# A two-layer backbone on one core: token-side norm behind the feed-forward, six modulation tiles moved to the router, pair parameters a step early

## What is computed

```
x = x + gate * rms_norm(sublayer(modulate(x, norm_pre, shift, scale)), norm_post)
```

## Time and profile before

| | |
|---|---|
| median of 3 runs | 1936.82 us (1935.96 to 1938.35) |
| profiled execution | 1934.04 us |
| its span | 1932.3 us |
| mean granted TensorE clock | 0.954 |
| busy: PE, VectorE, ScalarE, GpSimd | 1767.5, 1284.7, 985.6, 132.3 us |
| HBM read, written | 438.99 MB, 2.62 MB |

### The profile page before, as it was taken

One profiled execution on the slowest core, in us unless ns is written; L12 is line 12 of the kernel. 1 busy time (PEld: TensorE's weight loads), 2 busy tenths in 40 slices (PEclk: granted clock), 3 DMA queues, 4 the chain that ended last, 5 costly groups with the idle time before them and its releaser, 6 DMA issues.

```text
span 1932.3 us, 32651 instructions
## 1 busy us (share of the span) xinstructions
PE 1767.5 (91%) x11466; PEld 1430.8 (74%) x11466; DVE 1284.7 (66%) x1889; ACT 985.6 (51%) x1356; POOL 132.3 (7%) x208
## 2 busy tenths in 40 slices
PE   4989999977979998898669999999999999999997
PEld 2757777756768884797558788887878787878785
DVE  4345666665255551322379898989888898989897
ACT  1322222221234443122248787877777777878684
POOL 0134333330000000110000000000000000000000
PEclk8889999988989998899869999999999999999999
DMA  9531111020755437433339898988989797979790
GB/s 402 211 142 41 41 41 41 3 90 17 316 228 183 152 135 290 152 135 135 155 119 370 302 366 315 369 333 344 351 326 370 295 372 298 379 303 367 307 351 22
DMA packets 61367, 442.86 MB, mean 229 GB/s; under 512 B 7008, under 2 KB 8160, under 8 KB 10080
## 3 DMA queue, kind: packets, MB, share of 16 engines
q1 hardware_dynamic: 59184, 437.81, 59.3%
q10 hardware_dynamic: 1584, 2.79, 0.4%
q0 software_dynamic: 512, 1.05, 0.2%
HBM read 438.99 MB, written 2.62 MB: 229 GB/s over the span
## 4 chain that ended last, share of the span: by engine, by line
PE 81%; DVE 8%; issue 4%; DMA 3%; ACT 2%; POOL 1%; DVEq 0%; ACTq 0%; POOLq 0%; SPq 0%
PE PS L865 33%; PE PS L894 17%; PE PS L616 4%; PE PS L953 3%; PE PS L593 3%; PE PS L1044 2%; PE PS L699 2%; PE PS L1067 2%; PE PS L573 2%; PE PS L557 2%; DMA MIX<-w_mod 2%; PE PS L958 1%; PE PS L882 1%; DVE LO L1501 1%; PE PS L679 1%
## 5 line engine op out<-in xcount | busy, mean ns | idle before, releaser
L1501 DVE TENSOR_TENSOR LO<-W,HI 128x1024 fp32r<-128x1024 f32 x662 | 781.9, 1222 | 111.7 <-ACT HI L1101 65.2
L1101 ACT ACTIVATE HI<-W 128x1024 fp32r<-128x1024 f32 x662 | 689.7, 1062 | 137.4 <-PE PS L865 77.5
L865 PE MATMUL PS<-HI,XHI 128*128 128x512 f32 x970 | 393.5, 406 | 16.4 <-ACT XHI L1300 14.1
L865 PE MATMUL PS<-HI,XLO 128*128 128x512 f32 x970 | 380.6, 392 | 0.0
L865 PE MATMUL PS<-LO,XHI 128*128 128x512 f32 x970 | 294.8, 393 | 9.1 <-DVE LO L1501 8.5
L865 PEld LDWEIGHTS PS<-HI,XHI 128*128 128x128 f32 x970 | 183.1, 189 | 55.6 <-issue 15.8
L865 PEld LDWEIGHTS PS<-LO,XHI 128*128 128x128 f32 x970 | 181.3, 188 | 55.6 <-DVE LO L1501 16.3
L865 PEld LDWEIGHTS PS<-HI,XLO 128*128 128x128 f32 x970 | 183.5, 189 | 34.9
L894 PE MATMUL PS<-HI,HHI 128*128 128x512 f32 x484 | 188.9, 390 | 1.5 <-ACT HHI L1277 1.5
L894 PE MATMUL PS<-HI,HLO 128*128 128x512 f32 x484 | 188.3, 389 | 0.0
L894 PE MATMUL PS<-LO,HHI 128*128 128x512 f32 x484 | 145.5, 389 | 0.0
(11 more groups left out here) (285 smaller groups left out, 2160.0 us busy)
## 6 DMA issues: line engine op xcount, KB each, us to landing
W<-w_exp SPq DMA_DIRECT2D x298, 1024.0 KB, 6.9
W<-w_ffn SPq DMA_DIRECT2D x33, 1024.0 KB, 4.9
W<-w_mod SPq DMA_DIRECT2D x32, 1024.0 KB, 13.0
MIX<-w_mod SPq DMA_DIRECT2D x16, 1024.0 KB, 16.8
W<-w_rkv SPq DMA_DIRECT2D x8, 1792.0 KB, 8.2
W<-w_qkv SPq DMA_DIRECT2D x8, 1536.0 KB, 7.9
W<-w_o SPq DMA_DIRECT2D x1, 4096.0 KB, 12.0
W<-w_o SPq DMA_DIRECT2D x1, 3072.0 KB, 11.1
```

The source lines that it names most:

```text
L865: last = mm(PS[2 * (s % 2) + g], x[:, 2 * n + k, T * g:T * g + T], w[:, 512 * k:512 * k + 512], start=(n == 0 and k == 0 and i == 0 and le ...
L1101: fn(HI[:, u % NBUF], raw_unit(phase, u), ACT.Copy).then_inc(hi_ready, 1)
L1501: tt(LO[:, u % NBUF], raw_unit(phase, u), HI[:, u % NBUF].bitcast(F32), ALU.subtract)\
```

## The change

1. Layer 1's tiles 6 to 11 leave the stretch before attention. Their 12 blocks go to five buffers in MIX; SP issues five when the feed-forward is through and seven at the router, in front of the expert loads that need the output weights' place. TensorE runs tiles 6 to 9 in front of `norm_sum(7)` and tiles 10, 11 behind it.
2. Behind the feed-forward the post norm is made with tokens on partitions: ScalarE squares the four banks with a running sum (NSUM), makes a root for two columns (NROOT), VectorE a reciprocal; ScalarE and VectorE scale the banks into YNAT; TensorE turns them; VectorE adds them to XT straight from PSUM with the gain. `norm_sum(4)` is gone.
3. `norm_pre` works and signals by quarters of two chunks (`h_quarter`), for the feed-forward also the low part; attention's first product and the router's turning wait for quarters.
4. In the RWKV steps PP is copied at the end of the step before; TensorE runs `right_side` ahead of `prep_coef`, and `prep_hat` behind `solve0`; VectorE masks one gram in front of the hat copy. The last two steps of VectorE's loop are written out.
5. In an expert job one split stands ahead of the gathered copies on ScalarE and VectorE.

```diff
 # TensorE, mix_step
                 if ahead is not None:
                     prep_gate(ahead[2])
+                right_side(c, p)
                 if prep is not None:
                     prep_coef(prep[0])
-                    prep_hat(prep[0])
-                right_side(c, p)
                 for n, f in enumerate((solve0, solve1, solve2)):
                     if prep is not None:
                         gram(n % 2, prep[0], prep[1], 1 + n // 2)
                     for e in range(2):
                         f(e, c, p)
+                    if prep is not None and n == 0:
+                        prep_hat(prep[0])
...
 # VectorE
-            def prep_params(c, r, p):
+            def prep_params(c, p):
+                cs = slice(c, c + 1) if isinstance(c, int) else bass.ds(c, 1)
+                if not isinstance(c, int) or c >= 2:
+                    dve.wait_ge(prep_pool, 3 * (c - 2) + 3)
+                    dve.wait_ge(prep_act, 4 * (c - 2) + 2)
+                nc.vector.tensor_copy(PP[p].unsqueeze(1), PAIR[:, cs]).then_inc(prep_dve, 1)
...
                     prep_bonus(*prep[:2])
+                    gram(0, prep[0], 1 - p, 1)
                     prep_hat(*prep[:2])
-                    gram(0, prep[0], 1 - p, 1)
+                    if more:
+                        prep_params(prep[0] + 1, p)
                     gram(1, prep[0], 1 - p, 1)
...
+            def norm_pre(n, l, k, split_low=False):
+                dve.wait_ge(root_ready, seq(n))
                 order(nc.vector.reciprocal(RSTD, RMS))
-                order(tt(B[1], XT, RSTD.unsqueeze(1).to_broadcast([P, C, TT]), ALU.mult))
-                norm_shift(l, k)
+                for b in range(4):
+                    part = B[1][:, 2 * b:2 * b + 2]
+                    order(tt(part, XT[:, 2 * b:2 * b + 2], RSTD.unsqueeze(1).to_broadcast([P, 2, TT]), ALU.mult))
+                    norm_shift(l, k, range(2 * b, 2 * b + 2)).then_inc(h_quarter, 1)
+                    if split_low and b:
+                        low_quarter(b - 1)
+                if split_low:
+                    low_quarter(3)
...
 # SP
-            for late in range(MOD_LOADS - 2 * EARLY):
-                if late < 7:
-                    sp.wait_ge(lo_ready, UNITS["ffn"] + 2 * (FFN_LOADS - 6 + late))
-                else:
-                    sp.wait_ge(mod_used, MOD_LOADS + 2 * EARLY + late - 6)
+            for late in range(2 * (MIDDLE - EARLY)):
+                sp.wait_ge(lo_ready, UNITS["ffn"] + 2 * (FFN_LOADS - 6 + late))
                 load("late", late, a["w_mod"][1, 2 * EARLY + late])
-                if late == 8:
-                    attention_start()
-            sp.wait_ge(mod_used, 2 * MOD_LOADS)
+            attention_start()
+            sp.wait_ge(lo_ready, UNITS["exp"])
             sp.dma_start(W[:, WO1:W_COLS], a["w_o"][1]).then_inc(wo_full[1], 16)
+            sp.wait_ge(lo_used, UNITS["exp"])
+            def last_tiles(lo, hi):
+                for late in range(lo, hi):
+                    if late >= LATE:
+                        sp.wait_ge(mod_used, MOD_LOADS + 2 * MIDDLE + late - LATE + 1)
+                    m = 2 * MIDDLE + late
+                    sp.dma_start(mod_block(1, m), a["w_mod"][1, m]).then_inc(late_full[late % LATE], 16)
+            last_tiles(0, LATE)
...
                 if slot("exp", m) == WO1 // LOAD:
+                    last_tiles(LATE, MOD_LOADS - 2 * MIDDLE)
                     sp.wait_ge(wo_psum[1], 4)
...
 # ScalarE, behind the feed-forward
-                    last = fn(YNAT[:, g, 512 * half:512 * half + 512], PS[4 + 2 * g + half], ACT.Copy)
-            last.then_inc(yn_sbuf, 1)
+                    last = fn(flat[0][...], PS[4 + 2 * g + half], ACT.Square, accum_out=NSUM[:, g, half:half + 1])
+            last.then_inc(nsum_act, 1)
+            act.wait_ge(nsum_dve, 1)
+            fn(NROOT, NSUM[:, :, 0], ACT.Sqrt, scale=1.0 / D, bias=BIASES[:, 0:1]).then_inc(nsum_act, 1)
+            act.wait_ge(nsum_dve, 2)
+            for half in range(2):
+                fn(YNAT[:, 0, 512 * half:512 * half + 512], PS[4 + half], ACT.Copy, scale=NROOT[:, 0:1])\
+                    .then_inc(yn_act, 1)
...
 # ScalarE and VectorE, expert job
                 hidden(NS - 1)
+                split("exp", 2 * FFN_LOADS, j)
                 gathered(j + 1)
-                split("exp", 2 * FFN_LOADS, j)
                 split("exp", 2 * FFN_LOADS + 1, j)
```

More of the change, by code:

```diff
@@ L206, in mod_block @@
         def mod_block(l, m):
-            if l == 0 and m >= 2 * EARLY:
-                at = (m - 2 * EARLY) % LATE * LOAD
+            first = 2 * (MIDDLE if l else EARLY)
+            if m >= first:
+                at = (m - first) % LATE * LOAD
                 return MIX[:, at:at + LOAD]
@@ L363, in build @@
         loads, had = {}, [0] * RING
-        for name, n in (("mod0", 2 * EARLY), ("mod1", 2 * EARLY), ("ffn", FFN_LOADS), ("late", MOD_LOADS - 2 * EARLY),
+        for name, n in (("mod0", 2 * EARLY), ("mod1", 2 * EARLY), ("ffn", FFN_LOADS), ("late", 2 * (MIDDLE - EARLY)),
                         ("exp", 0)):
@@ L377, in mod_arrived @@
         def mod_arrived(eng, l, m):
-            late = m - 2 * EARLY
-            if late < 0:
+            late = m - 2 * (MIDDLE if l else EARLY)
+            if m < 2 * EARLY:
                 arrived(eng, f"mod{l}", m)
-            elif l:
-                arrived(eng, "late", late)
-            else:
-                eng.wait_ge(late_full[late % LATE], 16 * (late // LATE + 1))
+            elif late < 0:
+                arrived(eng, "late", m - 2 * EARLY)
+            else:
+                turns = sum((x - late) % LATE == 0 for x in range(MOD_LOADS - 2 * EARLY)) if l else 0
+                eng.wait_ge(late_full[late % LATE], 16 * (late // LATE + 1 + turns))
         def mod_bank(l, t):
@@ L576, in norm_part, with norm_sum @@
                     last.then_inc(sum_ready, 1)
-            def norm_sum(n, chunks=range(4)):
-                for i, b in enumerate(chunks):
-                    norm_part(n, i, b, B[1])
+            def norm_sum(n, squares=B[1]):
+                for b in range(4):
+                    norm_part(n, b, b, squares)
             def project_out(l, src):
@@ L1010, in _ @@
             project_out(1, B[1])
+            modulation(1, MIDDLE, 10)
             norm_sum(7)
-            pe.wait_ge(h_ready, 3)
-            for g in range(G):
-                for c in range(C):
+            pe.wait_ge(mod_ready, 5)
+            modulation(1, 10, MOD_TILES)
+            for c in range(C):
+                if c % 2 == 0:
+                    pe.wait_ge(h_quarter, 8 + c // 2 + 1)
+                for g in range(G):
                     last = nc.tensor.transpose(PS[2 * g + c // 4][:, P * (c % 4):P * (c % 4) + P],
                                                HT[:, c, T * g:T * g + T], IDENT)
-            last.then_inc(hn_psum, 1)
+                if c % 4 == 3:
+                    last.then_inc(hn_psum, 1)
             rw = col("router_w").rearrange("p (c e) -> p c e", c=C)
@@ L1359, in _ @@
             wo_out(1)
-            norm(7, XT)
-            act.wait_ge(hn_psum, 1)
+            rows(1, MIDDLE, 8)
             for b in range(4):
+                act.wait_ge(x_ready, 8 + b + 1)
+                square(b, XT[:, 2 * b:2 * b + 2])
+                if b < 2:
+                    rows(1, 8 + b, 9 + b)
+            norm_root(7)
+            rows(1, 10, MOD_TILES)
+            for b in (0, 2, 1, 3):
+                if b < 2:
+                    act.wait_ge(hn_psum, b + 1)
                 fn(HNHI[:, b // 2, 512 * (b % 2):512 * (b % 2) + 512], PS[b], ACT.Copy).then_inc(hn_sbuf, 1)
@@ L1532, in norm_shift @@
                                   MOD[:, l, (0 if k == 0 else 3) * C + c, g:g + 1], ALU.mult, ALU.add)
-                    if quarter is not None and c % 2:
-                        last.then_inc(quarter, 1)
-                if quarter is None:
-                    last.then_inc(h_ready, 1)
+                return last
             def norm_post(n, l, k, src, order=order):
-                dve.wait_ge(root_ready, n)
+                dve.wait_ge(root_ready, seq(n))
                 order(nc.vector.reciprocal(RSTD, RMS))
```

140 lines of the change are left out of this document (75 added, 65 removed).

## The result

The changed kernel takes 1893.89 us (median of 5 runs, 1883.25 to 1894.06) against 1936.82 (5 runs, 1934.02 to 1938.66): a ratio of 0.977, 95% interval 0.974 to 0.979. The forecast was 1889, range 1878 to 1903. Its runs fall into two groups, one of 1883.25 and four of 1892.57 to 1894.06; the execution profiled first is that of 1883.25, and one of the second group was profiled in the first experiment (1892.70), so both can be read.

The account below looks back on a forecast made before the run. Bound mostly by TensorE in feed-forward and expert lines; the change targets stretches where TensorE stands. Steps -14.3, feed-forward start -3.3, end -34, router +4 make -47.6: 1934.0 becomes 1886.4, plus 2.8 is 1889 us, range 1878 to 1903.

Parts of the forecast that it names:

- Steps: RWKV steps: copying parameters earlier frees GpSimd's keys, and the right side runs while GpSimd works; minus 14.3 us, bounds 8 and 24.
- A charge of 0: RWKV steps: swapping hat copy and first mask on VectorE changes the order, not the work; 0 us.
- Clock in the steps: Rival for the RWKV steps: with the pauses gone TensorE keeps 2.4 GHz; 1879 us in all, chance 0.10.
- The upper bound: RWKV steps: at most TensorE's 2.62 us stall and 1.8 of lost clock go, 4.4 per step; 2.0 was taken.
- Keys beside other work: RWKV steps: GpSimd's keys now run beside VectorE masks that read PSUM; charged 0, at most 1.9 us.
- Start of the feed-forward: Before the feed-forward: norm, shift, high and low part by quarters start it earlier; minus 3.3 us, bounds 2.5 and 3.5.
- End of the feed-forward: Between feed-forward and attention: moved tiles and token-side norm let attention start sooner; minus 34 us, bounds 32 and 37.
- The rival that the token norm wins nothing: Behind the feed-forward: its wait chain is as long as the old norm, some 20 of 34 us; 1903, chance 0.04.
- Router: Router: moved tiles' blocks delay the norm sum, quarters win back 2.5 us; net plus 4, bounds minus 1 and plus 12.
- the forecast's own sign: Router: the forecast is wrong if that stretch grows by more than 12 us.
- The rival of late blocks: Router: blocks land in 16.8 us each under a full queue, some 8 us on the path; 1897, chance 0.08.
- Experts, attention, queues: Experts: moved split 0, bounds minus 4 and plus 4 us; attention charged 0, its loads issued ahead of weights and blocks.

Follow-up runs that it names:

- the first experiment: The changed kernel run again with no edit: 1888.63 us (4 runs), ratio 0.976 against the kernel before; profiled at 1892.70.

## Why the prediction was right, and where it was not

**Steps: right in mechanism, near in size.** From pair 1's low-rank product to the output projection 12.6 and 13.3 us were gained for 14.3. By steps: first 0.6 for 1.3, second 0.5 lost for 0, four steady ones 8.3 for 8.0, from the last preparing step to the projection 4.1 and 5.0 for 5. "What is late next is VectorE's mask of level 1, behind its tail" held: L717 waits for it, and moving the tail took 0.84 to 1.18 us more from each steady step. A charge of 0 was not 0, in the steady steps and in the second: the changed order costs 0.5 per step, since VectorE's idle time lies mostly ahead of the first mask (2.48 us with the old order, 0.77 behind it); against it stand the 2 us in the last preparing step. The 4.4 and 2.7 us gained ahead of pair 1 have no term and need none: in seven profiles of kernels that are the changed one up to there, that product starts between 119.40 and 126.00 us, with a granted clock from 110 to 130 us of 0.91 in the first case and 0.51 in the last, and the 123.79 of before (0.66) lies among them. What they gave towards the forecast is luck.

**Clock in the steps: the condition came, the price did not.** All steps were granted 1.00, as the rival asked, yet they take 44.0 and not 41.7. The upper bound added the whole stall of 2.62 to a lost clock of 1.8. Of the stall, 0.74 stayed as a wait for VectorE and 0.5 went to the order. Of the lost clock some 0.7 came back, the fall of TensorE's busy time in a steady step from 42.71 to 41.98. Together that makes the 2.1 us per step that were won. The forecast had let everything in the 3.7 us at 1.2 GHz run at half speed, but the products there do not all take twice as long. In the kernel before, 32 products of 64 columns take 1.47 us at a granted 1.00 and 1.92 behind the stall of the earlier trace rows, at 0.50:

```profile
182.62 1.47 PE L689 MATMUL PS<-W,MIX 64*64 64x64 f32 x32
264.03 1.92 PE L689 MATMUL PS<-W,MIX 64*64 64x64 f32 x32
```

**Keys beside other work: 0, as charged.** L1704 went from a median of 0.58, at most 0.64, to 0.43 us and the masks beside the keys kept 1.25 to 1.29. The Trainium skill (GPSIMD Engine Reference, Key points) says that GpSimd contends with VectorE's instructions of two SBUF inputs. The traces agree: the one of that kind was relieved, and those that read PSUM did not notice.

**Start of the feed-forward: right.** 2.6 to 2.9 us for 3.3, within the bounds; making it whole again gave back 2.5 to 2.9.

**End of the feed-forward: right, step by step.** 35.8 us for 34, and 19.4 us to attention for "about 20"; the first qk product ended at 740.9, 29.1 behind the feed-forward, for 31.5. Two small slips in its sum (736.3 for 736.5, 744 for 745) lie within the bounds. The rival that the token norm wins nothing falls by 8.8 us.

**Router: the blocks were right, the clock was left out.** Block 7 was to land 10.7 us behind the projection; its product began 10.9 behind it. The stretch grew by 4.6 us in the run of 1883.25, for plus 4, in part by luck: measured from the end of the projection, the norm sum ended 4.9 us later than before, for 6.6, and the quarters saved 0.9 behind it, for 2.5, since tile 11 held the transposes. In that of 1892.70 it grew by 12.4, just outside the bound of 12, and by the forecast's own sign that makes it wrong there. The four runs that make the median were not profiled; their times are those of this one. The mis-sized step is "half tile 1.9, row 0.6, turn and hop 1.5, norm sum 3.7 to 5.38" with the rest taken as before: turn, norm sum and logits ran at 1.2 GHz, 7.2 us. In all, the run of 1892.70 gained 41.3 us for 47.6: the router fell short by 8.4, and the start gave 2.7 that nobody had forecast. The rival of late blocks had a price of 8 us and the wrong cause. The Trainium skill (TensorE: Matmul & The Clock Gate, HAM oscillation) says, of a kernel with longer waits than these, that waits for data between bursts make the next burst start at half clock. The traces agree in kind. The forecast applied it to the steps, where pauses were removed, and not to the router, where the change puts pauses in. The length of the waits does not decide it: waits of 0.27, 0.52 and 1.40 us left TensorE at 2.4 GHz up to the end of the norm sum in one run, waits of 0.78, 0.53 and 1.34 brought 1.2 GHz in another. What tips it is open.

**Experts, attention, queues: 0, as charged.** The nine jobs changed by 0.3 and 1.4 us in the two profiles; putting the split back changed nothing beyond that spread.

## What to carry to other kernels

A constant that another engine needs early in a step belongs at the end of the step before, and then the next late thing on the same queue wants the same treatment: here the copy gave some 2 us per step, and the tail behind it about one more. When work moves into a stretch where TensorE waits for loads, price the stretch behind it at both clock levels, since much the same waits gave either here. Put a reduction on which everything waits ahead of the last transfer that it does not need.

## What the runs showed that was not expected

Two short stretches, the start of the RWKV loop and the router, set the spread of this kernel's runs; everywhere else two profiles agree to about 1 us.

Eight profiles have the changed router with its pauses unfilled: the two above, and those of the kernels with the parameters late, the order back, the feature-side norm, the tail early, the start whole and the expert split back. In three of them the norm sum took 3.70 us and the stretch from the output projection to the first expert product 91.8 to 92.3; in five it took 5.16 to 6.51 and the stretch 98.9 to 99.9. The waits do not part them. The first row is of the start whole, where they were 0.44, 0.50 and 1.33 us and the norm sum took 3.70; the second is of the parameters late, where they were 0.44, 0.52 and 1.32 and it took 6.51:

```profile
904.08 1.06 PE L575 MATMUL PS<-MIX,COND 128*32 128x512 f32 x8 [1.33 <-DMA MIX<-w_mod]
905.69 1.58 PE L575 MATMUL PS<-MIX,COND 128*32 128x512 f32 x8 [1.32 <-DMA MIX<-w_mod]
```

At the router a late transfer went with faster logits: in the run of 1883.25 tile 11's last block came 1.33 us late, the transposes then ran without a pause, and the logits took 3.73 us; the other two profiles of that kind have 3.73 and 3.82. With pauses of 0.63 to 1.10 us between the quarters the same logits took 6.8 in all eight profiles that had them: the five with the slow norm sum, the pauses filled, the norm sum first, and the early tail with the router's order. That the pauses between the quarters are the cause is not shown: with the logits by quarters they were gone, and the level was low all the same.
